# A two-block hybrid network on one core: the feed-forward layer's up products all in row form, three groups ahead, and half of its input turned through HBM

## The reference, cut to what matters

```python
h = rmsnorm(x, g_mix)
z = h @ w_in
...
mixed = jax.nn.sigmoid(ga) * ya + jax.nn.sigmoid(gb) * yb
x = x + mixed @ w_out

h2 = rmsnorm(x, g_mlp)
x = x + jnp.square(jax.nn.relu(h2 @ w_up)) @ w_down
return x
```

## Time and profile before

| what | value |
| --- | --- |
| median of 3 runs | 985.03 us (985.02 to 986.42) |
| the profiled execution, its own time | 985.84 us |
| its span, first to last instruction | 984.0 us |
| PE busy | 976.9 us (99% of the span), 5274 matmuls |
| DVE busy | 737.9 us (75%) |
| ACT busy | 502.8 us (51%) |
| DMA | 218.47 MB, mean 222 GB/s |

### The profile page before, as it was taken

The page is one execution under the profiler, slowest core; times in us unless marked ns, Lnnn a source line. Parts: engine busy times, 40 slices in busy tenths (PEclk is TensorE's granted clock), DMA queues, the critical chain, the costliest instruction groups (busy, mean ns, idle before and its releaser), DMA issues.

```text
span 984.0 us, 12962 instructions
## 1 busy us (share of the span) xinstructions
PE 976.9 (99%) x5274; PEld 820.5 (83%) x5274; DVE 737.9 (75%) x829; ACT 502.8 (51%) x597; POOL 131.5 (13%) x101
## 2 busy tenths in 40 slices
PE   9999999999999999999999999999999999999997
PEld 8888888888888888888888888888887899799696
DVE  5878886776565666678787777878877778789984
ACT  5656553454444455455563454444378464644252
POOL 0000000000000000000000030000000149269720
PEclk9999999999999999999999999999999999999999
DMA  9887796657887764697796668778864957445451
GB/s 361 300 277 278 235 277 201 211 172 226 260 261 228 222 227 137 192 304 246 234 282 216 210 187 287 216 214 253 244 228 143 296 187 252 143 168 155 113 193 43
DMA packets 134522, 218.47 MB, mean 222 GB/s; under 512 B 11328, under 2 KB 44096, under 8 KB 134208
## 3 DMA queue, kind: packets, MB, share of 16 engines
q1 hardware_dynamic: 134464, 217.66, 69.7%
HBM read 196.17 MB, written 19.14 MB: 219 GB/s over the span
## 4 chain that ended last, share of the span: by engine, by line
PE 99%; DVE 0%; ACT 0%; issue 0%; POOL 0%; DVEq 0%; ACTq 0%
PE bank L946 15%; PE bank L948 15%; PE bank L949 15%; PE bank L969 12%; PE bank L973 11%; PE bank L980 11%; PE bank L1309 3%; PE bank L1313 1%; PE bank L1626 1%; PE bank L1084 1%; PE bank L1434 1%; PE bank L1397 1%; PE bank L1061 1%; PE bank L1174 1%; PE bank L1613 1%; PE bank L971 1%
## 5 line engine op out<-in xcount | busy, mean ns | idle before, releaser
L2131 DVE TENSOR_TENSOR w_lo<-raw,w_hi 128x2048 fp32r<-128x2048 f32 (+1 forms) x78 | 178.4, 2291 | 72.6 <-ACT w_hi L1714 72.5
L2131 DVE TENSOR_TENSOR w_lo<-arena,w_hi 128x2048 fp32r<-128x2048 f32 (+1 forms) x79 | 181.3, 2304 | 49.7 <-ACT w_hi L1714 49.4
L1714 ACT ACTIVATE w_hi<-raw 128x2048 fp32r<-128x2048 f32 (+1 forms) x83 | 157.0, 1891 | 84.8 <-PE bank L949 72.0
L1714 ACT ACTIVATE w_hi<-arena 128x2048 fp32r<-128x2048 f32 (+1 forms) x79 | 149.5, 1892 | 91.1 <-PE bank L949 85.4
L946 PE MATMUL bank<-w_hi,hT 128*128 128x512 f32 (+1 forms) x336 | 129.3, 385 | 0.0
L949 PE MATMUL bank<-w_hi,hT 128*128 128x512 f32 (+1 forms) x320 | 122.8, 384 | 0.0
L948 PE MATMUL bank<-w_lo,hT 128*128 128x512 f32 (+1 forms) x320 | 122.8, 384 | 0.0
L969 PE MATMUL bank<-w_hi,hT 128*128 128x512 f32 (+1 forms) x304 | 116.8, 386 | 0.0
L973 PE MATMUL bank<-w_hi,hT 128*128 128x512 f32 (+1 forms) x304 | 116.2, 384 | 0.0
L2896 POOL TENSOR_TENSOR rstd<-mean,const 128x1 f32<-128x1 f32 (+1 forms) x16 | 9.1, 577 | 619.8 <-DVE mean L2140 452.0
L946 PE MATMUL bank<-w_hi,uT_hi 128*128 128x512 f32 x208 | 81.0, 389 | 0.0
(11 more groups left out here) (350 smaller groups left out, 1809.3 us busy)
## 6 DMA issues: line engine op xcount, KB each, us to landing
arena<-in_w_in SPq DMA_DIRECT2D x21, 1024.0 KB, 5.5
raw<-in_w_in SPq DMA_DIRECT2D x20, 1024.0 KB, 6.7
arena<-in_w_up SPq DMA_DIRECT2D x16, 1024.0 KB, 6.6
raw<-in_w_up SPq DMA_DIRECT2D x16, 1024.0 KB, 6.0
arena<-in_w_down SPq DMA_DIRECT2D x16, 1024.0 KB, 5.2
raw<-in_w_down SPq DMA_DIRECT2D x16, 1024.0 KB, 5.6
u_bounce<-arena SPq DMA_DIRECT2D x12, 512.0 KB, 4.9
arena<-u_bounce SPq DMA_DIRECT2D x48, 128.0 KB, 5.7
```

What stands on the lines that cost most here:

```text
L1714: act.activation(w_hi[:, p % SPLIT_RING, :, 0:n], raw_at(p)[:, :, 0:n], copy).then_inc(hi_ready, 1)
L2131: dve.tensor_tensor(w_lo[:, s, :, 0:n], raw_at(p)[:, :, 0:n], w_hi[:, s, :, 0:n].bitcast(F32), ALU.subtract).then_inc(lo_ready, 1)
```

## The change

On PE all eight up groups are in row form, and the order is up 0, up 1, up 2, down 0, up 3, down 1, ... up 7, down 5, down 6, down 7 (`MLP_STEPS`, 16 steps, numbered 0 to 15). Each engine runs one loop over these steps: SP stores a group's rows three steps after it and fetches them four after it (in its own order, which runs some pieces ahead); at step i DVE turns the rows of the group of step i - 2 between the two weight pieces that it splits there, and makes `uT_lo` behind the second of them. `u_bounce` becomes two tensors.

Of the layer's input, only columns 512 to 1023 are turned on PE, in 8 transposes (`turn_columns`), four inside the last products of the mixer (`mixed_last`) and four inside up 0 (`mlp_first`). Columns 0 to 511 are copied by ACT from `x` to `u_rows` (`x_copied`), stored, fetched and turned like the rows of a group (`X_ROWS`), and up 0 uses them in its second half.

```diff
-UP_PIECE = [PIECE_MLP] + [PIECE_MLP + 4 * f - 2 for f in range(1, F_GROUPS)]
-DOWN_PIECE = [PIECE_MLP + 4 + 4 * f for f in range(F_GROUPS - 1)] + [PIECE_MLP + 4 * F_GROUPS - 2]
+UP_AHEAD = 3
+MLP_STEPS = [("up", f) for f in range(UP_AHEAD)]
+for f in range(F_GROUPS):
+    MLP_STEPS += [("down", f)] + ([("up", f + UP_AHEAD)] if f + UP_AHEAD < F_GROUPS else [])
+UP_PIECE = [PIECE_MLP + 2 * MLP_STEPS.index(("up", f)) for f in range(F_GROUPS)]
+DOWN_PIECE = [PIECE_MLP + 2 * MLP_STEPS.index(("down", f)) for f in range(F_GROUPS)]
...
     def store_up(l, g):
-        for t in range(T):
-            sp.wait_ge(out_free[t], l * USES + USE_UP + g + 1)
-        store_rows(u_bounce.rearrange("(t p) n -> p t n", p=P), u_rows, rows_stored)
+        if g == X_ROWS:
+            sp.wait_ge(x_copied, T * (l + 1))
+        else:
+            for t in range(T):
+                sp.wait_ge(out_free[t], l * USES + USE_UP + g + 1)
+        store_rows(u_bounce[g % 2].rearrange("(t p) n -> p t n", p=P), u_rows, rows_stored)
     def fetch_up(l, g):
-        sp.wait_ge(rows_stored, 16 * (STORES * l + 2 * T + g))
-        if g == 1:
-            sp.wait_ge(up_lo, 2 * (l * F_GROUPS + 1))
-        else:
-            sp.wait_ge(blocks_turned, MOVES * l + 2 + g - 1)
-        fetch_blocks(u_moved, u_bounce, row_blocks)
+        sp.wait_ge(rows_stored, 16 * (STORES * l + 2 * T + g + 2))
+        sp.wait_ge(blocks_turned, MOVES * l + 2 + g + 1)
+        fetch_blocks(u_moved, u_bounce[g % 2], row_blocks)
...
-        for f in range(-2, F_GROUPS):
-            if l == DEPTH - 1 and f == 0:
+        for i, (kind, f) in enumerate(MLP_STEPS):
+            if l == DEPTH - 1 and i == 2:
...
-            if f >= 0:
-                for c in range(2):
-                    rows_f = ins["w_down"][l, f * COLS:(f + 1) * COLS, :]
-                    load(square_piece(rows_f, c, 0))
-            if 0 < f < F_GROUPS - 1:
-                store_up(l, f)
-            if f + 2 < F_GROUPS:
-                load(square_piece(ins["w_up"][l], f + 2, 0))
-            if 0 < f < F_GROUPS - 1:
-                fetch_up(l, f)
-            if f + 2 < F_GROUPS:
-                load(square_piece(ins["w_up"][l], f + 2, 1))
+            for c in range(2):
+                if kind == "down":
+                    load(square_piece(ins["w_down"][l, f * COLS:(f + 1) * COLS, :], c, 0))
+                else:
+                    load(square_piece(ins["w_up"][l], f, 1 - c if f == 0 else c))
+                if c == 0 and i >= 4 and MLP_STEPS[i - 4][0] == "up":
+                    fetch_up(l, MLP_STEPS[i - 4][1])
+            if i == 1:
+                store_up(l, X_ROWS)
+                fetch_up(l, X_ROWS)
+            if i >= 3 and MLP_STEPS[i - 3][0] == "up":
+                store_up(l, MLP_STEPS[i - 3][1])
+        fetch_up(l, F_GROUPS - 1)
...
+        tokens_out(l * USES + USE_UP + f, l * PIECES + UP_PIECE[f], 2, hT_hi, hT_lo)
+    def turn_columns(l, t):
+        pe.wait_ge(out_free[t], l * USES + USE_O + 2)
+        for b in range(2):
+            for k in (KP + 2 * b, KP + 2 * b + 1):
+                c = (k % 2) * P
+                last = pe.transpose(ROWS_T[2 * t + b][:, c:c + P], x[:, t, k * P:(k + 1) * P], ident)
+            last.then_inc(turned, 1)
+    def mixed_last(l):
+        n, p = l * USES + USE_O + 1, l * PIECES + PIECE_O + 2
+        def parts(i, t):
+            at, s = slice(t * P, (t + 1) * P), (p + i) % SPLIT_RING
+            return [(OUT[t], hT_hi[:, i * KP + kk, at], hT_lo[:, i * KP + kk, at], w_hi[:, s, kk, :], w_lo[:, s, kk, :], False)
+                    for kk in range(KP)]
+        pe.wait_ge(hi_ready, p + 1)
+        out_ready(n, 0)
+        products_upper(parts(0, 0), p, True, False)
+        out_ready(n, 1)
+        products(parts(0, 1), True, False).then_inc(piece_used, 1)
+        pe.wait_ge(hi_ready, p + 2)
+        products_upper(parts(1, 0), p + 1, False, True).then_inc(out0_done, 1)
+        second = parts(1, 1)
+        products(second[:2], False, False)
+        turn_columns(l, 0)
+        products(second[2:], False, True).then_inc(piece_used, 1)
...
+    def mlp_first(l):
+        for t in range(T):
+            out_ready(n, t)
+            if t == 0:
+                pe.wait_ge(hi_ready, p + 1)
+            for b in range(2):
+                pe.wait_ge(turned_hi, turns + 2 * t + b + 1)
+                part(w_hi, hT_hi, 0, t, first=True, blocks=(2 * b, 2 * b + 1))
+            if t == 0:
+                piece_ready(p)
+            part(w_lo, hT_hi, 0, t)
+            if t == 0:
+                turn_columns(l, 1)
+            pe.wait_ge(turned_lo, turns + 2 * t + 2)
+            last = part(w_hi, hT_lo, 0, t)
+        pe.wait_ge(hi_ready, p + 2)
+        pe.wait_ge(up_hi, l * ROWS_MOVED + 1)
+        part(w_hi, hT_hi, 1, 0)
+        pe.wait_ge(up_lo, l * ROWS_MOVED + 1)
+        part(w_hi, hT_lo, 1, 0)
+        piece_ready(p + 1)
+        part(w_lo, hT_hi, 1, 0, last_one=True).then_inc(out0_done, 1)
+        part(w_hi, hT_hi, 1, 1)
+        part(w_hi, hT_lo, 1, 1)
+        part(w_lo, hT_hi, 1, 1, last_one=True).then_inc(piece_used, 1)
...
-        tokens_out(l * USES + USE_O + 1, l * PIECES + PIECE_O + 2, 2, hT_hi, hT_lo)
-        turn_rows(x, lambda t: out_free[t], lambda t, i: l * USES + USE_O + i // 2 + 1)
-        mlp_up(l, 0)
-        mlp_up_rows(l, 1)
-        for f in range(F_GROUPS):
-            if l == DEPTH - 1 and f == F_GROUPS - 1:
+        mixed_last(l)
+        mlp_first(l)
+        for kind, f in MLP_STEPS[1:]:
+            if kind == "up":
+                mlp_up(l, f)
+            elif l == DEPTH - 1 and f == F_GROUPS - 1:
                 mlp_last(l)
             else:
                 mlp_down(l, f)
-            if f + 2 < F_GROUPS - 1:
-                mlp_up_rows(l, f + 2)
-            elif f + 2 < F_GROUPS:
-                mlp_up(l, f + 2)
 
...
     def up_rows_out(l, f):
-        act.wait_ge(up_lo, 2 * (l * F_GROUPS + f))
+        act.wait_ge(up_lo, l * ROWS_MOVED + 1 + (f if f >= UP_AHEAD else max(f - 1, 0)))
         for t in range(T):
             whole(act, l * USES + USE_UP + f, t)
             act.activation(relu_buf[:, t, :], OUT[t], ACT.Relu).then_inc(up_half, 1)
     def up_rows_upper(l, f):
-        act.wait_ge(blocks_turned, MOVES * l + 2 + f)
+        act.wait_ge(blocks_turned, MOVES * l + 2 + f + 2)
         if f >= 2:
             act.wait_ge(piece_used, l * PIECES + DOWN_PIECE[f - 2] + 2)
         k = (f % 2) * HALF
-        act.activation(uT_hi[:, k:k + HALF, :], u_turned, copy).then_inc(up_hi, 2)
+        act.activation(uT_hi[:, k:k + HALF, :], u_turned, copy).then_inc(up_hi, 1)
...
+        step(p + PIECE_O)
+        step(p + PIECE_O + 1)
+        act.wait_ge(rows_stored, 16 * (STORES * l + 2 * T))
+        for t in range(T):
+            act.wait_ge(out_free[t], l * USES + USE_O + 1)
+            act.activation(u_rows[:, t, :].rearrange("p (b s f) -> p s b f", b=BLOCKS, f=BLOCK),
+                           x[:, t, 0:COLS].rearrange("p (s b f) -> p s b f", b=BLOCKS, f=BLOCK), copy).then_inc(x_copied, 1)
+        for t in range(T):
+            squares(2 * l + 1, t, 0)
+        step(p + PIECE_O + 2)
+        step(p + PIECE_O + 3)
+        columns_hi(l, 0)
+        step(p + PIECE_MLP)
+        columns_hi(l, 1)
+        act.wait_ge(blocks_turned, MOVES * l + 2 + 1)
+        for k in range(KP):
+            last = act.activation(hT_hi[:, k, :], u_turned[:, k, :], copy, scale=vec[:, V_MLP + KD * l + k:V_MLP + KD * l + k + 1])
+        last.then_inc(up_hi, 1)
+        for t in range(T):
+            act.wait_ge(out_free[t], l * USES + USE_O + 2)
+            squares(2 * l + 1, t, 1)
+        for i, (kind, f) in enumerate(MLP_STEPS):
+            if i:
+                step(p + PIECE_MLP + 2 * i)
+            if i >= 2 and MLP_STEPS[i - 2][0] == "up":
+                up_rows_upper(l, MLP_STEPS[i - 2][1])
+            if l < DEPTH - 1 or i < len(MLP_STEPS) - 1:
+                step(p + PIECE_MLP + 2 * i + 1)
+            if kind == "up":
+                up_rows_out(l, f)
+            elif l == DEPTH - 1 and f in (F_GROUPS - 3, F_GROUPS - 2):
...
     def up_rows_turn(l, f):
-        dve.wait_ge(row_blocks, 16 * BLOCKS * (MOVES * l + 2 + f))
+        dve.wait_ge(row_blocks, 16 * BLOCKS * (MOVES * l + 2 + f + 2))
+        if l or f != X_ROWS:
+            dve.wait_ge(up_lo, l * ROWS_MOVED + f + 1)
+        for t in range(T if f != X_ROWS else 0):
+            dve.wait_ge(out_free[t], l * USES + USE_UP + (f if f >= UP_AHEAD - 1 else f + 1) + 1)
         turn_blocks(u_turned, u_moved, HALF).then_inc(blocks_turned, 1)
     def up_rows_lower(l, f):
-        dve.wait_ge(up_hi, 2 * (l * F_GROUPS + f + 1))
+        dve.wait_ge(up_hi, l * ROWS_MOVED + f + 2)
         k = (f % 2) * HALF
-        dve.tensor_tensor(uT_lo[:, k:k + HALF, :], u_turned, uT_hi[:, k:k + HALF, :].bitcast(F32), ALU.subtract)                   .then_inc(up_lo, 2)
```

(57 more changed lines are left out.)

152 lines of the change are left out of this document (37 added, 115 removed).

## The result

The change takes **1004.05 us** (median of 5 executions, 1002.85 to 1008.01) where the kernel before takes 985.27 beside it: a ratio of 1.019, 95% interval 1.017 to 1.021, slower by 18.8 us. The forecast was 7.1 slower, with 996.3 as its upper end. The direction was right and the size was not.

What follows compares the result with a forecast made beforehand. The prediction took PE, busy for 99% of the span, as the bound. Its terms, -4.0 + 4.0 + 1.6 + 4.0 + 0.6 + 0.9 = +7.1 us, on the median of 985.03 gave 992.1 us, range 987.8 to 996.3.

Steps and rivals of the forecast that it cites:

- PE's own work: On PE: row form for up 0 and up 7, fewer transposes and shorter `uT_lo` waits gain 4.0 us.
- The input through HBM: First 512 input columns, stored and fetched: in time for the turn with 1.1 us of cover, so no cost.
- The start of up 1: PE waits for a free bank while DVE finishes its work: 0.3 us a layer, 0.6 in sum.
- Down 0: Third step of each layer: `uT_lo` of up 0 comes late, a gap of 2.0 us a layer, 4.0 in sum.
- Down 7 of layer 0: Step 15 of layer 0: `uT_lo` of up 7 comes late, a gap of 1.6 us.
- Down 7 of layer 1: Last down group: late `uT_lo` after the sine, plus DVE falling behind; 4.0 us, bounds 2.9 and 5.5.
- the lag: DVE in layer 1: 22.9 us of work per 21.8 us pair of steps, falling behind about 1 us each pair.
- The small tables: Layer 1, step 2 on SP: the store of squares stands behind weight loads, up 2 waits 0.9 us, bounds 0 and 2.
- The clock: Rival: PE's clock halves after the long gap, twenty slow matmuls add 4.5 us, 996.6 us; chance 0.08.
- Faster: Rival: `uT_lo` is not late at down 0 and down 7, 981.0 to 982.5 us; chance 0.05.
- Only the fixed sequence counts: Rival: DVE doesn't lag, tables and start of up 1 cost nothing; +4.5 us, 989.5 us; chance 0.26.
- The rows come late: Rival: rows through HBM late by 1 us in each layer and for down 0; 996.1 us; chance 0.10.

Runs made afterwards that it cites:

- e3: The change with layer 1's small tables fetched ahead of step 5's weights instead of step 2's; 1007.88 us, ratio 1.023.
- e13: The change with SP's four fetches of a step put ahead of both weight loads of that step; 998.38 us, ratio 1.013.
- e1: The change with `uT_lo` made ahead of the second weight split on DVE; 988.97 us, ratio 1.003.
- e10: e8 with SP's four fetches of a step put ahead of both weight loads of that step; 982.88 us, ratio 0.998.
- e8: e7 with the second sine on ACT moved behind the layer's last groups, into the next mixer; 988.28 us, ratio 1.003.
- e15: e10 with the small tables fetched at step 2 again, as in the change; 986.01 us, ratio 1.001.
- e16: e10 with both sines where the change has them; 985.99 us, ratio 1.001.
- e7: The change with the edits of e1 and e3 together: `uT_lo` ahead of the second split, small tables at step 5; 993.2 us, ratio 1.007.
- e6: The kernel before with `uT_lo` moved behind the second weight split on DVE; 999.87 us, ratio 1.014.
- e12: e8 with the small tables at step 2 and the second weight copy and split ahead of the turn and `uT_hi`; 1002.21 us, ratio 1.017.
- e4: The change with layer 1's angles two parts behind each of five down steps instead of one behind every step; 1006.9 us, ratio 1.022.

## Why the prediction was wrong, and where it was right

- **PE's own work, -4.0 forecast, -3.7 measured.** The walk through start times holds.
- **The input through HBM, forecast nothing.** The turn of these blocks started at 202.89 right behind the work ahead of it, and PE went on with no wait. Right. On DVE:

```profile
201.86 1.11 DVE L2550 SCALAR_TENSOR_TENSOR hT<-bank,vec,hT 128x128 fp32r<-128x128 f32 x4
202.89 1.23 DVE L2324 STREAM_TRANSPOSE arena<-arena 128x1024 f32<-128x1024 f32 x1
```

- **The start of up 1, 0.6 forecast, 0.8 measured** (gaps of 0.26 and 0.23, each with its restart). Right.
- **Down 0, 2.0 a layer forecast.** Measured 2.4 in layer 0. The mechanism is the forecast one, as the timeline of DVE shows, which answers to the earlier trace rows:

```profile
229.47 1.25 DVE L2324 STREAM_TRANSPOSE arena<-arena 128x1024 f32<-128x1024 f32 x1 [0.69 <-DMA arena<-u_bounce]
233.65 2.29 DVE L2148 TENSOR_TENSOR w_lo<-raw,w_hi 128x2048 fp32r<-128x2048 f32 x1 [2.93 <-ACT w_hi L1727]
235.86 1.22 DVE L2392 TENSOR_TENSOR uT_lo<-arena,uT_hi 128x1024 fp32r<-128x1024 f32 x1
```

  The turn waited 0.69 us for its blocks, which I had given 1 us to spare. In e3, with the same layer 0, it started at 228.78 without waiting and the gap was 1.45: that is the fixed sequence, 2.0 forecast. In layer 1 down 0 had no gap of its own, since up 2 was already 3 us late.
- **Down 7 of layer 0, 1.6 forecast, 1.2 measured.** Right in kind, with the same half microsecond too much.
- **Down 7 of layer 1, 4.0 forecast with 5.5 as its bound; 7.65 measured** over the three gaps at 700, 747 and 761. This step failed. Its fixed part held: 2.9 forecast for down 7 itself, 2.65 measured at 761. What was mis-sized is the lag, taken as 1.1 us with 2.6 as its most, and measured as 5.0 at 700 and 747. (The bound was low by its own count too: three pairs of steps at 22.9 - 21.8 = 1.1 us make 3.3, which over 2.9 is 6.2 and not 5.5.) I added up DVE's instructions of two steps (22.9 us) and took the excess over 21.8 as the lag. The round isn't that sum but a ring of waits through DVE, ACT, SP and the DMA queues, 23.6 to 26.2 us: through the shared area of `relu_buf` and `u_turned`, a load that waits for a split, and the fetch's landing of 6.4 to 8.8 us. With the fetch first (e13) the rounds, 21.7 to 23.2 us, come down to about what I had counted for DVE; the rest of the change's rounds was the way over SP and the transfers. e1 shortens the ring by what stands ahead of `uT_lo`, e10 by what stands ahead of the fetch. I had also looked for the lateness at `uT_lo` alone; two of three times the split was late, behind the angles.
- **The small tables, 0.9 forecast (0 to 2), 3.2 measured.** The mechanism was the forecast one and the size was off. I took 597.5 us for the landing of the store. On SP two of the table loads took 4.08 and 2.42 us to issue, the store went out at 591.53 behind the weight loads, and DVE had its landing and could start the squares only 12 us later, at 603.67 (3.8 us of that lateness against 597.5 is layer 0's, the rest the tables'):

```profile
579.45 0.36 SPq L833 DMA_DIRECT2D arena<-in_g_final  x1
...
580.80 4.08 SPq L836 DMA_DIRECT2D arena<-in_o_c_im  x1
584.92 2.42 SPq L838 DMA_DIRECT2D arena<-in_o_b_re  x1
...
591.53 2.00 SPq L729 DMA_DIRECT2D u_bounce<-arena  x1
```

- **The clock, a rival at 0.08 with 4.5 us for one gap of 4 us.** It happened, 1.6 us at a time, but five times, since gaps of little over 2 us were enough. This is the second step that failed: the forecast's own sum had nothing for the clock, and it cost 8 us. The rule of the Trainium skill ("TensorE: Matmul & The Clock Gate", Part 1) that an idle PE is throttled to half its clock and released by activity is borne out by this trace's windows at 0.50. That rival and the lag of layer 1 were kept apart in the working, though each gap that the lag makes calls on the clock.
- **The other rivals.** *Faster* fell. *Only the fixed sequence counts* holds in layer 0 alone. *The rows come late* is the 0.69 us above; the input's rows were on time.

How the two positions share the loss is settled by runs as far as they go: 15 us for `uT_lo` alone, 6 us for the fetch alone, and 5.4 us for the fetch on top of the others (e8 to e10). No run has these two edits and nothing else. An estimate from e10, e15 and e16 is 982.9 + 3.1 + 3.1 = 989.1, which is e1's time; so the two aren't additive, which fits two edits that shorten one ring. What is left open: why e7 is slower than e1, and why it varies between 989.2 and 995.1 while e10 stays within 982.7 and 984.4. The clock alone doesn't explain it: e7's fastest execution had a mean granted clock of 0.997, and one of 993.3 us had 0.999. Its one trace is of the fastest execution, and shows gaps of 1.0 and 3.1 us.

## What to carry to other kernels

Where operands go out through HBM and come back, write down the ring (buffer reuse, engine order, queue order, landing) and compare its length with PE's time for one round; an engine's busy sum alone doesn't give it. On every engine and queue put what the ring needs (the read that frees its buffer, its fetch) ahead of what only has to be there a step later, and expect that a gap of over 2 us on PE may cost another 1.6 us behind it. If removing one gap moves the loss elsewhere, stop removing gaps and look for the ring.

## What the runs showed of the hardware

- In the two layers and at the transposes right behind them, over all traces, the granted clock never fell at a gap of up to 1.94 us (e15) and always at one of 2.56 or more. In between, from 2.03 us (e16) to 2.53 us (e6), it went either way, so the length alone didn't decide: in e12 the same gap, of 2.46 us, was followed by 0.50 at down 0 and by 1.00 throughout at down 7 (windows of 2 us).

```profile
238.00:240.00 2.00, 2.00 (x7) 1.51 (x6) 1.27 (x2) 2.00 (x2) 0.00 (x0) 0.50 0.93 198
...
370.00:372.00 2.00, 0.00 (x0) 0.00 (x0) 1.06 (x1) 2.00 (x2) 0.00 (x0) 1.00 0.91 299
372.00:374.00 2.00, 1.78 (x8) 1.47 (x9) 1.42 (x2) 0.71 (x1) 0.00 (x0) 1.00 0.54 210
```

- When the level falls differs from gap to gap. In the change, behind 761.16 six matmuls come at 0.22 to 0.34 us from one another, and only from 762.67 on are they 0.43 apart; behind 237.13 the very first ones are slow. In e4, in the gap of 6.68 us up to 758.69, it fell while PE still stood:

```profile
756.00:758.00 2.00, 0.00 (x0) 0.00 (x0) 2.00 (x2) 2.00 (x1) 0.00 (x0) 0.50 0.00 0
```
- A store behind four 1 MB weight loads took 12 us to be seen as landed, where such stores take 3.7 us in the median of this kernel.
